# Zero stores three loads later, separate first token lists, and an early square-root table, in a transformer step with grouped experts

## What is computed

```python
def grouped_moe(h, w_router, b_router, w_gate, w_up, w_down):
    t = h.reshape(B * L, D)
    aff = jax.nn.sigmoid((t @ w_router).astype(jnp.float32))
    sel = aff + b_router.astype(jnp.float32)
    gscore = lax.top_k(sel.reshape(-1, N_GROUPS, EXPERTS_PER_GROUP), 2)[0].sum(-1)
    gbest = jnp.argmax(gscore, axis=-1)
    in_group = (jnp.arange(N_EXPERTS) // EXPERTS_PER_GROUP)[None, :] == gbest[:, None]
    _, idx = lax.top_k(jnp.where(in_group, sel, -jnp.inf), TOP_K)
    wsel = jnp.take_along_axis(aff, idx, axis=-1)
    wsel = wsel / jnp.sum(wsel, axis=-1, keepdims=True)
    gate = jnp.sum(jax.nn.one_hot(idx, N_EXPERTS, dtype=jnp.float32) * wsel[..., None], axis=1)
    hid = jax.nn.silu(jnp.einsum('td,edf->tef', t, w_gate)) * jnp.einsum('td,edf->tef', t, w_up)
    y = jnp.einsum('tef,efd->td', hid * gate[:, :, None].astype(hid.dtype), w_down)
    return y.reshape(B, L, D)
```

## Time and profile before

| What | Value |
|---|---|
| Runs of the kernel before | 751.68 us median of 3 (749.96 to 753.31) |
| The profiled execution, its own time | 752.79 us |
| Its span in the trace | 750.9 us |
| Mean granted TensorE clock | 0.964 of full |
| Busy: TensorE, VectorE, ScalarE, GpSimd | 90%, 30%, 21%, 20% of the span |
| Chain of waits by engine | TensorE 83%, DMA 6%, VectorE 5%, SP's queue 2% |
| Moved by DMA | 186.17 MB, 248 GB/s on average |

### The profile page before, as it was taken

One profiled execution on the slowest core, in us unless ns is written; L12 is line 12 of the kernel. 1 busy time (PEld: TensorE's weight loads), 2 busy tenths in 40 slices (PEclk: granted clock), 3 DMA queues, 4 the chain that ended last, 5 costly groups with the idle time before them and its releaser, 6 DMA issues.

```text
span 750.9 us, 11852 instructions
## 1 busy us (share of the span) xinstructions
PE 673.5 (90%) x4923; PEld 412.1 (55%) x4923; DVE 226.1 (30%) x505; ACT 159.3 (21%) x330; POOL 151.2 (20%) x186
## 2 busy tenths in 40 slices
PE   0899999997999999999989999999999999999600
PEld 0656556564458888544477546566546654654400
DVE  0510099900034554232377101111101011110157
ACT  4202210201146675211221011010111001111042
POOL 5107840900033450031111100000100000000040
PEclk9999999998999999999998999999999999999955
DMA  9986860994039430074172899979999999994184
GB/s 249 385 271 128 242 225 1 347 332 175 1 122 390 190 115 2 0 292 184 65 301 70 282 358 326 383 275 400 380 390 392 417 360 412 407 410 176 45 288 131
DMA packets 50663, 186.17 MB, mean 248 GB/s; under 512 B 7152, under 2 KB 9577, under 8 KB 46384
## 3 DMA queue, kind: packets, MB, share of 16 engines
q1 hardware_dynamic: 43408, 163.18, 59.0%
q0 software_dynamic: 7088, 22.17, 9.0%
q10 hardware_dynamic: 112, 0.04, 0.0%
HBM read 163.13 MB, written 22.31 MB: 247 GB/s over the span
## 4 chain that ended last, share of the span: by engine, by line
PE 83%; DMA 6%; DVE 5%; SPq 2%; ACT 1%; issue 1%; POOL 1%; POOLq 0%; DVEq 0%; ACTq 0%
PE bank L1728 11%; PE bank L1735 10%; PE bank L1584 9%; PE bank L1465 7%; PE bank L1751 6%; PE bank L1760 5%; PE bank L1525 5%; PE bank L1412 4%; PE bank L1626 4%; DMA slots<-in_w_ada 3%; PE bank L1428 3%; PE bank L1743 3%; PE bank L1470 2%; PE bank L1715 2%; SPq L444 2%; DMA x<-in_x_prompt 2%
## 5 line engine op out<-in xcount | busy, mean ns | idle before, releaser
L1465 PE MATMUL bank<-ra,slots 128*128 128x512 f32 x192 | 83.3, 594 | 0.4 <-DVE ra L843 0.4
L1584 PE MATMUL bank<-slots,rc 128*128 128x512 f32 x160 | 69.9, 593 | 0.0
L1465 PEld LDWEIGHTS bank<-ra,slots 128*128 128x128 f32 x192 | 36.1, 190 | 45.6 <-issue 44.6
L1154 DVE TENSOR_TENSOR rc<-re,bank 128x256 f32<-128x256 f32 (+1 forms) x32 | 10.2, 359 | 160.8 <-PE bank L1735 88.5
L1353 POOL COPY gi<-ridx 128x1 uint32<-128x1 uint32 x18 | 3.6, 198 | 272.8 <-PE bank L1715 237.7
L1728 PE MATMUL bank<-rb,rc 128*128 128x512 f32 x128 | 56.2, 595 | 0.0
L858 DVE SCALAR_TENSOR_TENSOR re<-re,cwT 128x670 f32<-128x670 f32 x60 | 52.3, 945 | 0.0
L554 ACT ACTIVATE rb<-bank 128x512 f32<-128x512 f32 (+1 forms) x64 | 31.1, 525 | 94.7 <-PE bank L1465 49.6
L1584 PEld LDWEIGHTS bank<-slots,rc 128*128 128x128 f32 x160 | 29.9, 190 | 34.9 <-issue 34.9
L1735 PE MATMUL bank<-slots,rc 128*64 128x256 f32 x384 | 43.7, 382 | 0.0
L1241 POOL TENSOR_TENSOR mod<-mod,vecT 128x8 f32<-128x8 f32 (+1 forms) x8 | 19.6, 2455 | 117.9 <-ACT mod L554 117.9
(11 more groups left out here) (296 smaller groups left out, 989.2 us busy)
## 6 DMA issues: line engine op xcount, KB each, us to landing
slots<-in_w_ada SPq DMA_DIRECT2D x12, 2048.0 KB, 12.5
slots<-in_moe_w_gate SPq DMA_DIRECT2D x8, 2048.0 KB, 12.7
rb<-in_moe_w_gate SPq DMA_DIRECT2D x8, 2048.0 KB, 11.4
rb<-in_moe_w_up SPq DMA_DIRECT2D x8, 2048.0 KB, 14.5
rb<-in_moe_w_down SPq DMA_DIRECT2D x8, 2048.0 KB, 12.2
slots<-in_moe_w_up SPq DMA_DIRECT2D x8, 2048.0 KB, 14.5
slots<-in_moe_w_down SPq DMA_DIRECT2D x8, 2048.0 KB, 14.1
slots<-in_w_in SPq DMA_DIRECT2D x4, 2048.0 KB, 14.0
```

What stands on the lines that cost most here:

```text
L1465: ins = mm(b[:, :], w[:, k, m * P:(m + 1) * P], hT[:, k, 0:NLAT], start=k == 0, stop=k == KD - 1)
L1584: ins = mm(b[:, :], mT[:, k, i * P:(i + 1) * P], wo[k // 4][:, k % 4, 512 * hf:512 * hf + 512], start=k == 0, stop=k == KD - 1)
```

## The change

Three edits. The zero stores move from ahead of load 12 to ahead of load 15. The token lists of experts 0 and 1 become two lists, each made in a bank of its own from the ranks of all tokens (`rank`) and from a token number that is zero where the token did not choose the expert, and not from the picked ranks; the sums over earlier tiles, which VectorE made, become five matmuls with ones that add onto the triangular one; GpSimd gathers by `ridx` itself for these two; fillers are cut from 8, 18, 8 to 4, 12, 4. And ScalarE takes one square root of a used value before the tail's first gather.

```diff
-    plan += [(("rank",), "D"), (("first",), "D"), (("table",), "D")]
+    plan += [(("rank",), "D"), (("first", 0), "D"), (("first", 1), "D"), (("table",), "D")]
...
-            if n == 12:
+            if n == 15:
 
                 sp.wait_ge(S["zeros_ready"], 1)
...
+        sc.activation(ss[:, 1, 0:1], ss[:, 1, 0:1], ACT.Sqrt)
         gate(0)
...
-        link(v.tensor_tensor(sel2, hot[:, 0], hot[:, 1], ALU.add))
-        v.memset(before[:, 0:NE], 0.0)
-        link(v.tensor_copy(before[:, NE:2 * NE], sel2[:, 0:NE]))
-        for c in range(1, TT):
-            ins = v.tensor_tensor(before[:, (c + 1) * NE:(c + 2) * NE], before[:, c * NE:(c + 1) * NE],
-                                  sel2[:, c * NE:(c + 1) * NE], ALU.add)
-            if c < TT - 1:
-                link(ins)
-        ins.then_inc(S["route_ready"], 1)
+        v.memset(sel2[:, n:n + NE], 0.0)
+        v.tensor_tensor(sel2[:, 0:n], hot[:, 0], hot[:, 1], ALU.add).then_inc(S["route_ready"], 1)
...
-        rank, rows = cnt, misc[:, 0:NE]
-        v.tensor_copy(rows, b[:, 2 * n:2 * n + NE])
-        link(v.tensor_copy(rank, b[:, 0:n]))
-        v.tensor_tensor(rank, rank, b[:, n:2 * n], ALU.add).then_inc(S["evac_d"], 1)
+        ranks = pa_[:, 224:224 + n + NE]
+        rank, rows = ranks[:, 0:n], ranks[:, n:]
+        evac(ranks, b[:, 0:n + NE])
...
+        v.tensor_tensor(firsthot, three(sel2[:, 0:n])[:, :, 0:2], K("tok").unsqueeze(2).to_broadcast([P, TT, 2]),
+                        ALU.mult).then_inc(S["tiles_hot"], 1)
+        for e in range(2):
+            v.tensor_tensor(rowhot[:, e * TT:(e + 1) * TT, :], K("iota").unsqueeze(1).to_broadcast([P, TT, P]),
+                            three(rank)[:, :, e].unsqueeze(2).to_broadcast([P, TT, P]), ALU.is_equal).then_inc(S["rows_hot"], 1)
         pick(rk, three(rank))
-        rows_of(rk)
+        b = filled(dve, "first", 0)
+        evac(ridx[:, 0:1], b[:, 0:1])
...
-        gather(0, 0)
-        gather(1, 1)
+        for b in range(2):
+            emptied(pool, "first", b)
+            g.indirect_dma_start(xg[:, b, :], None, t["h2d"],
+                                 bass.IndirectOffsetOnAxis(ap=ridx[:, b:b + 1], axis=0)).then_inc(xg_in[b], 16)
...
-        mm(b[:, 0:n], K("tri"), sel2, start=True, stop=True)
-        give(mm(b[:, n:2 * n + NE], K("ones"), before, start=True, stop=True))
-        keep_warm(8)
+        mm(b[:, 0:n + NE], K("tri"), sel2, start=True, stop=False)
+        for c in range(TT):
+            w = TT - c
+            ins = mm(b[:, (c + 1) * NE:n + NE].rearrange("p (a e) -> p a e", a=w), K("ones"),
+                     sel2[:, c * NE:(c + 1) * NE].unsqueeze(1).to_broadcast([P, w, NE]), start=False, stop=c == TT - 1)
+        give(ins)
+        keep_warm(4)
...
-        keep_warm(18)
-        emptied(pe, "first")
+        keep_warm(12)
+        emptied(pe, "first", 1)
...
-            keep_warm(8)
+            keep_warm(4)
```

More of the change, by code:

```diff
@@ L277, in build @@
     tilehot = rb[:, 13568:13568 + 10 * NT].rearrange("p (b n) -> p b n", b=10)
-    firsthot = rb[:, 14100:14120].rearrange("p (a e) -> p a e", e=2)
+    firsthot = rb[:, 14100:14110].rearrange("p (a e) -> p a e", e=2)
     before = rb[:, 13568 + 10 * NT:13568 + 10 * NT + (TT + 1) * NE]
@@ L960, in _ @@
         sel, cnt, hot = W[:, 0:n], W[:, n:2 * n], rw[:, n:3 * n].rearrange("p (k n) -> p k n", k=2)
-        sel2, tmp = W[:, 2 * n:3 * n], W[:, 3 * n:4 * n]
+        sel2, tmp = pb_[:, 160:160 + n + NE], W[:, 3 * n:4 * n]
         misc = W[:, 4 * n:4 * n + 64]
@@ L1036, in rows_of @@
                                 at_row[:, k].unsqueeze(2).to_broadcast([P, TT, P]), ALU.is_equal).then_inc(S["rows_hot"], 1)
+        v.tensor_tensor(firsthot, three(sel2[:, 0:n])[:, :, 0:2], K("tok").unsqueeze(2).to_broadcast([P, TT, 2]),
[3 more added lines that the diff above has]
+                            three(rank)[:, :, e].unsqueeze(2).to_broadcast([P, TT, P]), ALU.is_equal).then_inc(S["rows_hot"], 1)
         pick(rk, three(rank))
-        v.tensor_tensor(firsthot.rearrange("p (k i) e -> p k i e", k=2),
-                        hot.rearrange("p k (i e) -> p k i e", i=TT)[:, :, :, 0:2],
-                        K("tok").unsqueeze(1).unsqueeze(3).to_broadcast([P, 2, TT, 2]), ALU.mult).then_inc(S["tiles_hot"], 1)
-        rows_of(rk)
+        b = filled(dve, "first", 0)
+        evac(ridx[:, 0:1], b[:, 0:1])
         tab = room[:, 0:48].rearrange("p (t e) -> p t e", t=3)
@@ L1053, in _ @@
         link(v.tensor_reduce(order, pairs, AX.X, ALU.add))
-        b = filled(dve, "first")
-        evac(ridx[:, 0:2], b[:, 0:2])
+        b = filled(dve, "first", 1)
+        evac(ridx[:, 1:2], b[:, 1:2])
         link(v.tensor_scalar(late, order, 4.0, -32.0, ALU.is_ge, ALU.mult))
@@ L1346, in _ @@
         pool.wait_ge(h2_out[1], 16 * 2)
-        emptied(pool, "first")
         def gather(b, tile):
@@ L1353, in gather @@
             g.tensor_copy(gi[:, b:b + 1], ridx[:, at_n]).then_inc(S["gi_ready"], 1)
-            pool.wait_ge(S["gi_ready"], tile + 1)
+            pool.wait_ge(S["gi_ready"], tile - 1)
             pool.sem_inc(S["gi_seen"], 1)
@@ L1680, in _ @@
         n = TT * NE
-        sel2 = ra[:, 4736 + 2 * n:4736 + 3 * n]
+        sel2 = pb_[:, 160:160 + n + NE]
         keep_warm(21)
@@ L1684, in _ @@
         b = take("rank")
-        mm(b[:, 0:n], K("tri"), sel2, start=True, stop=True)
-        give(mm(b[:, n:2 * n + NE], K("ones"), before, start=True, stop=True))
-        keep_warm(8)
-        pe.wait_ge(S["tiles_hot"], 1)
[L1689 to L1694, removed]
-        keep_warm(18)
-        emptied(pe, "first")
+        mm(b[:, 0:n + NE], K("tri"), sel2, start=True, stop=False)
[5 more added lines that the diff above has]
+        keep_warm(4)
+        pe.wait_ge(S["tiles_hot"], 1)
+        for e in range(2):
+            b = take("first", e)
+            pe.wait_ge(S["rows_hot"], e + 1)
+            for q in range(TT):
+                ins = mm(b[:, 0:2], rowhot[:, e * TT + q, :], firsthot[:, q, :], start=q == 0, stop=q == TT - 1)
+            give(ins)
+        keep_warm(12)
+        emptied(pe, "first", 1)
         def table():
```

## The result

The changed kernel takes 769.25 us (median of 4 runs, 768.82 to 769.60) against 752.15 us (4 runs, 749.96 to 753.31) for the kernel before: a ratio of 1.0231, 95% interval 1.0206 to 1.0255, 17.1 us slower. The profiled execution took 768.82 us with a span of 766.9 us, 16.0 more than before. The prediction said 767.0 us, 760 to 774, slower. Its sum on the profiled execution was 768.0; 768.82 was measured.

A forecast was written before the change was run, and what follows sets the result against it. TensorE was taken to bound the kernel, so only its stops and slow stretches count. Terms -6.9 + 27.6 + 1.5 - 5.7 - 1.3 = +15.2 us on 752.79 gave 768.0, or 767 at the median; range 760 to 774.

The forecast's parts named there:

- The wait given back: Modulation matmuls near 169.6 us: TensorE's 4.84 us wait for load 12 and the slow clock after it go, -6.9 us.
- The exponential behind the zeros: Attention: ScalarE's first exponential waits until the zeros have left the shared buffer, +27.6 us.
- T: Moment SP issues load 14, once the last value projection frees its slot: 217.15 us before, 210.2 predicted after.
- TensorE's idle time and restart: Attention: TensorE idles some 20 us during ScalarE's wait and restarts at the low clock, +1.5 us.
- Load 15: Load behind the zeros: lands near T + 44, 254.2 us, wanted at 258.8, so hidden by 4.6 us.
- T + 44 less T + 21: Load 15's predicted landing, less when TensorE would want it were there no wait on ScalarE.
- Routing: From ranks to first expert: earlier list and gather give 4.9 us, 8 fewer filler passes 0.9; -5.7 us taken.
- The weakest choice, the clock: Routing: full clock assumed because idle time ahead of the list matmuls is shorter; at low clock only 2.7 us gained.
- The tail: End of kernel: the square-root table load moves into ScalarE's wait for gathers, -1.3 us.
- Hidden zeros: Rival: load 14 and zeros go out while DMA engines idle, 182 to 217 us; -13.9, 738 us; chance 0.03.
- Zeros at full rate: Rival: narrow stores keep 421 GB/s, zeros out at T + 29.2, 6.8 us less, 760 us; chance 0.13.
- Longer stall: Rival: zeros take until T + 39, or routing's low clock stays; +3 us each, 770 to 774; chance 0.17.

The follow-up runs named there:

- u1: Changed kernel with the zero stores back ahead of load 12, new token lists and early table load kept: 746.50 us, ratio 0.9938 to the kernel before.
- u4: Changed kernel with the zeros written from a buffer of their own, still queued behind load 14: 764.84 us, ratio 1.0191 to the kernel before.
- p4: Kernel before with only the fillers cut from 8, 18, 8 to 4, 12, 4: 751.30 us, ratio 0.9988.
- p2: Kernel before with the new token lists and the fewer fillers, zeros and table load unchanged: 748.07 us, ratio 0.9952.
- p5: Kernel before with the new token lists and the fillers left at 8, 18, 8: 750.07 us, ratio 0.9972.
- p3: Kernel before with the early square-root table load alone: 750.57 us, ratio 0.9983.
- u3: Changed kernel with the zero stores issued before SP waits for load 14's slot: 740.10 us, and 739.58 in a second group; ratios 0.9861 and 0.9844.
- u5: Changed kernel with zeros from a buffer of their own, queued behind all weight loads of the stage: 739.30 us, ratio 0.9835 to the kernel before.

## Why the prediction came out right, point by point

**The wait given back (-6.9 predicted, -6.8 measured).** Both of its pieces are gone, the 4.84 us and the slow clock; u1 brings them back. What was named as next, the column sums and the value products, followed without a gap.

**The exponential behind the zeros (+27.6 predicted, +28.2 measured).** The zeros were to be out at T + 36 and were out at T + 36.55; the exponential came at T + 36.57 in place of T + 8.4. The method held: take the same queue with the same load ahead of it, and measure in the trace before how long the stores needed. The bound of T + 29.2, all stores at 421 GB/s, was wrong for the reason given with it, the narrow stores: 215 GB/s after, 212 before. The Trainium skill says why such a rate is to be expected ("SBUF — State Buffer", Door 1: The DMA port swizzle): 32 or 64 partitions from the first on reach the same half of the 16 ports. By it an estimate would be half of 435 GB/s, 217; the trace agrees with 212 and 215.

**TensorE's idle time and restart (+1.5 predicted, 1.4 measured).** The stage grew by 29.6, the exponential's delay is 28.2, so 1.4 are left; they fit the low clock from 246 to 252 and were not measured apart. "About 20 us of TensorE idle" was too small: it stopped at 220.3, earlier than assumed, and stood 26.80. That changed no term, since the end of the wait is set by the zeros.

**Load 15 (hidden by 4.6 predicted).** It landed at 228.32 + 24.9 = 253.2 (254.2 had been predicted) and was used at 260.10: hidden by 6.9. "Should the zeros be quicker, this load becomes the next wall" is what u4 shows: 23.09 us of wait, against T + 44 less T + 21.

**Routing (-5.7 predicted, -4.5 measured): the mis-sized term.** Its steps, with the 21.97 us taken off by which the router started later: the list was to be read by 392.1 and was by 414.26 - 21.97 = 392.29; the gather was to be issued at 392.25 and went at 393.14; the rows were to be there at 396.55, and the transposes began at 397.60. The wrong step is "GpSimd's copy of the list goes too: it issues the gather at 392.25". I took the 0.86 us between copy and gather for something that goes with the copy. It stays: 0.79 us without a copy, 0.82 with one. Between list and gather stand 0.85 us where the forecast has 0.15; that is 0.7 of the 1.2 us. The rest is small: 0.2 us for the list (VectorE lets 0.40 us pass between the rank matmuls and their copy), 0.14 of issue between the gather's landing and the transposes, and 0.24 for transposes that took 1.12 us in place of 0.88. (These make 1.3, since the forecast's 4.9 and 0.9 are 5.8 and not 5.7.) The lead of the gather with a copy ahead of it, in p4's chain:

```profile
396.62 0.20 POOL gi L1353
396.85 0.82 issue
```

**The weakest choice, the clock.** The reason given for it, a shorter idle time ahead of the list matmuls, was wrong. That time was 0.69 us before and 0.81 in the kernel after:

```profile
391.69 2.78 PE L1693 MATMUL bank<-rb 128*128 128x2 f32 x20 [0.69 <-DVE rb L1035]
...
412.73 2.37 PE L1694 MATMUL bank<-rb 128*128 128x2 f32 x20 [0.81 <-DVE rb L1034]
```

The clock stayed up in the kernel after all the same; it fell in u1 and p2 behind the same 0.81 us, and in p5 without any. What decides it no run here shows, and that it came out as chosen was luck. Nothing depended on it, though. "If the clock falls as before, … only 2.7 are left" is refuted by u1 and p2: the clock did fall there, and the stage still lost 4.4 and 4.3 us. I had let the 16 passes behind the gather (transposes and fillers) run at the low level for 3.5 us; in u1 they take 2.02, since the clock is back at 1.00 by 397 us.

**The tail (-1.3 predicted, -1.4 in the traces, -1.3 in p3).** Right.

**The rivals.** "Hidden zeros" (738) was the right mechanism in a place where this kernel does not issue them; u3 does, and gives 739.6 to 740.1, higher by 1.6 to 2.1 us, of which 1.2 are the routing. u5 gives the same from the other side, 739.3. The zeros out at T + 36.55 rule out "Zeros at full rate" (T + 29.2) and "Longer stall" (T + 39), whose other condition, a low clock in the routing, did not come.

**From the sum to the median.** 767.0 is 2.25 below 769.25: 0.8 from the sum, 1.1 because the profiled execution before lay that much above its median, and 0.4 because the profiled one after lay below its own. That the sum is only 0.8 off is in part luck. Its terms came out 1.7 us too low together (1.2 of them the routing, 0.5 the stall), and the 0.9 us of scatter in the first stage hid half of that.

## What to carry to other kernels

The price of a bulk transfer is set by what is queued behind it and by who waits for its buffer. Look up both, and freeing the buffer alone only hands the wait to the next load (u4). Before moving it, find the stretch in which the DMA engines stand idle and issue it ahead of the wait that keeps the queue out of that stretch (u3), or behind the last load that anyone needs soon (u5). Filler matmuls put in to keep the clock up should be checked against the granted clock: here it fell with all of them in place (p5), and cutting them gained 0.9 us by itself (p4). That the cut gains more once the work that they cover ends sooner (1.5 us, p2 against p5) lies within the noise.

## What the runs showed of the hardware that had not been expected

GpSimd's lead before an indirect DMA does not belong to the operation before it. It is 0.79 us after a wait for VectorE and 0.82 after a copy, with 0.30 between two indirect DMAs in a row. What it consists of no run here shows.

Stores of 9.7 MB, at up to 415 GB/s, beside TensorE, VectorE, ScalarE and GpSimd at work cost the kernel no time that could be measured (u5 against u3: 739.30 and 739.58 us, and 80.05 and 80.04 us in the attention's stage).

TensorE's clock fell to its 1.2 GHz level while TensorE was at work without a gap (p5: busy 2.00 of 2.00 us at 1.00 from 391 on, 0.50 from 394 on). What set it off no run here shows.
